# Dot products of units 4 and 5 read the normed rows from SBUF instead of PSUM

## The chip, the cores and the metric

The kernel runs on one core of one Trainium2 chip. The metric is the device time of one execution in microseconds. Three runs of the kernel before took 4679.68, 4685.80 and 4688.55 us; their median is 4685.8 us.

## What is computed

One inference step of a two-layer backbone over two request groups: 128 context tokens (group 0) and 512 latent tokens (group 1). Each layer has a mixing half (an input projection, a gated linear recurrence and an attention, an output projection) and an expert half (PEER), which is the one that matters here. For each token the expert half picks 128 rows of a table `u` (8 heads of 16), takes their dot products with the normed token, and sums 128 rows of a table `v` with the resulting weights:

```
def peer(h, w_q, sub_keys, u, v):
    def block(xb):
        ...
        idx = jnp.take_along_axis(cand_i, best_pos, axis=-1)
        gate = jax.nn.softmax(best_s, axis=-1)
        ue = u[idx]
        act = jax.nn.gelu(jnp.einsum('td,thkd->thk', xb, ue).astype(jnp.float32), approximate=False)
        ve = v[idx]
        return jnp.einsum('thk,thkd->td', (gate * act).astype(xb.dtype), ve)
```

All is float32, and rows have 1024 elements.

## The kernel before

**Units.** The expert half is done in ten units of 128 tokens, numbered `u` = 0 to 9: unit 0 is the context tile of layer 0, units 1 to 4 are the four latent tiles of layer 0, unit 5 is the context tile of layer 1, units 6 to 9 the latent tiles of layer 1. A unit has two stages. In the *u stage*, 128 gathers each bring one row of table `u` for each of the 128 tokens (128 x 4 KB, 512 KB) into one of the ten slots of `ring`, and the vector engine (DVE) takes one dot product with each (`dots`, L1549 to L1557: 64 steps of two). In the *v stage*, 128 gathers bring rows of `v`, and the tensor engine (PE) sums them into `acc` in PSUM (L972). `gelu` stands between the stages, and `finish` (L1566) behind the v stage adds the result to `x`.

**Who issues what.** GpSimd (POOL) issues all gathers, in the order of the units, as indirect DMAs at L679. It waits until the slot has been read: by the dot ten places before (semaphore `gu`), or by the sum (`gv`). SyncE (SP) issues the weight tiles of 512 KB (L616) into `wring`, which has three slots; it waits until the tile three places before has been used.

**Order.** Each engine runs one fixed list of steps, `plan()` (L186), and skips the steps in which it has no part. While a unit does its dots, other work of the plan is spread between them. Beside the dots of unit 4 stand `norms(3, 0) + projections(3, 0)`: the input projection of three latent tiles of layer 1, 26 weight tiles (PE at L757 for the first 12, L763 for the other 14), each evicted from one of two PSUM buffers by ScalarE (ACT), with a DVE step at the end, `fgate` (L1291, L1294), that waits for the last eviction. `norms` are three DVE steps (L1269 to L1281), after 4, 10 and 16 dots. Beside the dots of unit 5 stand the same for the fourth tile, then the recurrence of that tile, which is mostly DVE work. DVE works in order, so a dot that the plan puts behind `fgate` waits for it.

**The operand of the dots.** ACT writes the normed rows of a unit into `h2`, two slots of 128 x 1024 in SBUF (L1041), ahead of the unit. At the start of each unit the step `("hp", u)` makes ACT copy them in two halves into `acc` in PSUM (`normed_rows`, L1190 to L1197). The first half waits for `xh` and the second for `xr`, which `finish` of the unit before raises when `acc` is free. The first dot waits for both copies (L1552). The dot is one custom DVE instruction with two tensor inputs, a slot of `ring` in SBUF and `acc` in PSUM; its 128 x 1024 product is written back to the slot and its sum is read out by a short second instruction.

Of the kernel before, what the change touches and what calls it, by code (L numbers as in the profile page):

```python
# [7 lines left out]
ALU = mybir.AluOpType  # L8
# [17 lines left out]
U0 = [sum(NT[:p]) for p in range(4)]  # L26
NU = sum(NT)
H, DK = 8, 64
QL, KVL, ROPE, DQ = 384, 256, 32, 96
SCALE = float(64 + 32) ** -0.5  # L30
NK, TOPK = 128, 16
# [13 lines left out]
MERGED = 5  # L45
LV = len(LEVELS) + 2
SHARED = {(1, 2), (3, 2)}
BATCHES = [[(0, 1)], [(0, 4)], [(0, 1)], [(0, 3), (3, 4)]]


# [14 lines left out]
def modulations(l, lo, hi):  # L65

    out = []
    for j in range(lo, hi):
        out.append((("ada", l, j), 1.5))
        if j % (3 * SECT) == 2 * SECT - 1:  # L70
            out.append((("adafin", l, j // (3 * SECT)), 1))
    return out


def norms(p, b):

    return [(("norm", p, t, 0), 8) for t in range(*BATCHES[p][b])]


def projections(p, b, lo=0, hi=N_IN):  # L80

    t0, t1 = BATCHES[p][b]
    out = [(("inp", p, b, j), 2 * max(1, (t1 - t0) * 0.9)) for j in range(lo, hi)]
    if hi == N_IN:
        out.append((("fgate", p, b), 4))
        out += [(("small", p), 0)] if b == 0 else []
        out += [(("rows", p), 0), (("latn", p), 3 + 3 * NT[p])] if b == len(BATCHES[p]) - 1 else []
    return out


def scans(p, t0, t1):

    return [(("hg", p, t, m), 4) for t in range(t0, t1) for m in range(LV)]
# [26 lines left out]
def served(p, t):  # L120

    return (t, t + 1) if (p, t) in SHARED else (t,)

# [13 lines left out]
def queries(p, t):  # L137

    return joined(p, t) + searched(p, t)
# [16 lines left out]
def spread(a, b, until=1.0):  # L156

    def placed(steps):
        total, at, out = sum(us for _, us in steps), 0.0, []
        for step, us in steps:  # L160
            out.append(((at + us / 2) / total, step))
            at += us
        return out

    merged = sorted([(x, 0, i, step) for i, (x, step) in enumerate(placed(a))]
                  + [(x * until, 1, i, step) for i, (x, step) in enumerate(placed(b))])
    return [step for _, _, _, step in merged]


def spread_pairs(a, b):  # L170

    return [(step, 3) for step in spread(a, b)]
# [10 lines left out]
    return spread(out + [heads[H]], beside), [(("u", u, c), 1) for c in range((H - 2) * share, NCU)]  # L183


def plan():  # L186

    def alone(steps):
        return [step for step, _ in steps]

    out = alone(modulations(0, 0, 2 * SECT) + norms(0, 0) + projections(0, 0))
    out += spread(scans(0, 0, 1), modulations(0, 2 * SECT, 3 * SECT))
    out += spread(keys_values(0) + spread_pairs(attention(0, 0), outputs(0)), modulations(0, 3 * SECT, N_ADA))
    out += alone([(("keys", 0), 0)] + opened(0))
    entry = {0: (0, 0, norms(1, 0) + projections(1, 0, 0, 20)), 1: (1, 0, attention(1, 1) + joined(1, 1)), 6: (3, 0, attention(3, 1) + joined(3, 1))}
    ahead = {1: spread_pairs(attention(1, 0), outputs(1)) + [(("keys", 1), 0)] + opened(1)}
    prompt_q = queries(2, 0)
    beside_u = {0: projections(1, 0, 20) + scans(1, 0, 1), 1: searched(1, 1)[:-2],
                2: spread_pairs(attention(1, 3), modulations(1, N_ADA // 2, N_ADA)) + queries(1, 2),
                3: keys_values(2) + spread_pairs(attention(2, 0), outputs(2)) + [(("keys", 1), 0), (("score", 1, 3, 0), 3), (("score", 1, 3, 1), 3)],  # L200
                4: norms(3, 0) + projections(3, 0),
                5: norms(3, 1) + projections(3, 1) + scans(3, 3, 4) + keys_values(3)[:6],
                6: searched(3, 1)[:-2], 7: attention(3, 3) + joined(3, 2)}
    beside_v = {0: scans(1, 1, 4) + keys_values(1),
                1: queries(1, 1)[-2:] + spread_pairs(choice(1, 1), spread_pairs(modulations(1, 0, N_ADA // 2), attention(1, 2))),
                2: spread_pairs(choice(1, 2), norms(2, 0) + projections(2, 0, 0, 20)) + projections(2, 0, 20)
                + scans(2, 0, 1),
                3: [(("keys", 2), 0)] + spread_pairs(choice(1, 3), prompt_q[:-2]) + prompt_q[-2:] + choice(2, 0),
                4: scans(3, 0, 3),
                5: keys_values(3)[6:] + spread_pairs(attention(3, 0), outputs(3)) + [(("keys", 3), 0)] + opened(3),  # L210
                6: queries(3, 1)[-2:] + spread_pairs(choice(3, 1), attention(3, 2)), 7: searched(3, 2) + choice(3, 2),
                8: [(("score", 3, 3, 0), 3), (("score", 3, 3, 1), 3)] + choice(3, 3),
                9: [(("y", u), 3) for u in range(NU - 5, NU - 1)]}
    dense = {0: 0.85, 5: 0.85}
    for u in range(NU):
        out += alone(ahead.get(u, []))
        rest = [(("u", u, c), 1) for c in range(NCU)]
        if u in entry:
            steps, rest = chosen_and_read(*entry[u])
            out += [("hp", u)] + steps  # L220
        else:
            out.append(("hp", u))
        out += spread(rest, beside_u.get(u, []), dense.get(u, 1.0))
        out.append(("gelu", u))
        out += spread([(("v", u, c), 1) for c in range(NCV)], beside_v[u], dense.get(u, 1.0))
        out.append(("fin", u))
    return out + [("y", NU - 1)]
# [15 lines left out]
def same_batch(p, t, other):  # L243

    return any(t0 <= t < t1 and t0 <= other < t1 for t0, t1 in BATCHES[p])

# [93 lines left out]
def after(step, name):  # L340

    return TALLY[PLACE[step] + 1].get(name, 0)
# [46 lines left out]
def build(nc, A, O):  # L389
    with ExitStack() as ctx:  # L390
# [6 lines left out]
        def sem(name):  # L397
# [49 lines left out]
        h2 = sb("h2", [P, 2, D])  # L447
# [46 lines left out]
        dot = sb("dot", [P, H * TOPK])  # L494
# [3 lines left out]
        acc = ps("acc", [P, D])  # L498
# [20 lines left out]
        C = {name: sem("s_" + name) for name in (  # L519
            "it",  # L520
            "ia",
            "id",
            "tp",
            "te",
            "td",
            "wu",
            "mods",
# [42 lines left out]
        def normed_home(p, t):  # L570

            return mT2 if (p, t - 1) in SHARED else mT

        def query_home(p, t, half):

            if (p, t - 1) in SHARED:
                return (o, V)[half][:, :, :].rearrange("p a b -> p (a b)")[:, 512:1536].rearrange("p (a t) -> p a t", t=P)
# [23 lines left out]
        def _(sp):  # L601
# [3 lines left out]
            for k, step in enumerate(PLAN):  # L605
# [22 lines left out]
                elif name == "rows":  # L628
                    p, = a
                    sp.wait_ge(C["it"], after(("inp", p, len(BATCHES[p]) - 1, N_IN - 1), "it"))  # L630
                    sp.dma_start(qrow[:, :], A["qrow"][PASSES[p][1]]).then_inc(s_row, 16)
# [59 lines left out]
        def _(pe):  # L691
# [55 lines left out]
            def project(k, p, b, j):  # L747
                t0, t1 = BATCHES[p][b]
                if j == 0:
# [252 lines left out]
        def _(act):  # L1002
# [15 lines left out]
            def norm(k, p, t, which):  # L1018
                g, l = PASSES[p]
                if t == 0:  # L1020
                    act.wait_ge(C["mods"], after(("adafin", l, which), "mods"))
                root(k, st[:, 2:3], st[:, 1:2])
                n = before(k, "tp")
                for i in range(2):
                    src = got_t(n + i)
                    for c in range(4):
                        kc = 4 * i + c
                        if which:
                            dst = normed_home(p, t)[:, kc, :]
                        else:  # L1030
                            dst = hT[:, kc, t * P:(t + 1) * P] if t < BATCHES[p][0][1] else hT1[:, kc, :]
                        ins = nc.scalar.activation(dst, src[:, c, :], ACT.Identity, scale=Am[:, l, which, kc, g:g + 1],
                                                   bias=mods[:, l, 3 * which * KC + kc, g:g + 1])
                    ins.then_inc(C["te"], 1)
                if which:
                    u = U0[p] + t
                    if u >= 2:
                        act.wait_ge(C["hp"], 2 * (u - 1))
                    for i in range(2):
                        src = got_t(n + 2 + i)  # L1040
                        copy(h2[:, u % 2, 512 * i:512 * (i + 1)].rearrange("p (c t) -> p c t", t=P), src)\  # L1041
                            .then_inc(C["te"], 1)
# [213 lines left out]
        def _(dve):  # L1256
            v = nc.vector
# [290 lines left out]

            def dots(k, u, c):  # L1549

                if c == 0:
                    dve.wait_ge(C["hp"], 2 * (u + 1))  # L1552
                for i in range(CU):
                    rows = landed(dve, "peer_u", u, c * CU + i)
                    n = c * CU + i
                    v.tensor_tensor_reduce(rows, rows, acc[:, :], 1.0, 0.0, ALU.mult, ALU.add, dot[:, n:n + 1])\  # L1556
                        .then_inc(C["gu"], 1)  # L1557

            def gelu(k, u):
# [137 lines left out]
```

## Time and profile before

| what | value |
|---|---|
| median of three runs | 4685.8 us |
| span of the profiled execution | 5196.0 us (the profile gives no time outside its span) |
| DVE busy | 2863.5 us, 55% |
| of it the dots, L1556 | 1487.5 us, 1280 instructions |
| PE busy | 2947.7 us, 57% |
| POOL busy | 2429.0 us, 47% |
| gathers (software DMA queue) | 1342.34 MB, 68.6% of the 16 DMA engines |
| weights and other loads (hardware queue) | 240.76 MB, 13.3% |

The profile is one execution under the hardware profiler; its times run from the first instruction of the span. It took 510.2 us longer than the median of the timed runs. Tables by stage list, for a stretch of time, how long each engine was busy, the clock granted to PE as a share of full speed, the busy share of the DMA engines, and the rate at which they moved data. In timelines, the text in brackets is how long the engine was idle before the row, and what ended that.

### The profile page before, as it was taken

To read this page: it belongs to the slowest core of one execution; us is meant where nothing else is said; L and a number is where in the kernel's file an instruction comes from. 1 tells how busy PE (TensorE), PEld (TensorE's weight loads), DVE (VectorE), ACT (ScalarE), POOL (GpSimd) and SP (SyncE) were. 2 spreads that over 40 slices of the span, in tenths; PEclk is the share of its full clock that TensorE was granted. 3 is DMA by queue.
4 is the path that set the end of the run, shared out by engine and by line. 5 is a ranking of instruction groups with operands and counts; after the bars stand their busy time and mean duration, and the time that the engine had idled before them with its cause. 6 is when DMAs were issued, how large, how long until landed. Compare 5 with 4: busy or idle time off the path is not lost. (4 is left out here: it accounts for less than half of the span.)

```text
span 5196.0 us, 51262 instructions
## 1 busy us (share of the span) xinstructions
PE 2947.7 (57%) x18894; PEld 1865.7 (36%) x18894; DVE 2863.5 (55%) x7112; ACT 607.1 (12%) x1305; POOL 2429.0 (47%) x2565
## 2 busy tenths in 40 slices
PE   6758667744677576237457643685466467025025
PEld 5545633634435453123136333253432353000000
DVE  1258572289247544776863458326935833873740
ACT  2210121210111011110101110211111110000000
POOL 0024154045354435555653643445446646566665
PEclk9579788656885698568678875786677577556556
DMA  6468477278899879899985987788789989899998
GB/s 213 147 232 337 148 267 269 92 277 333 312 382 360 303 266 367 345 360 369 348 343 195 335 329 243 259 333 326 301 319 359 358 306 361 326 359 366 363 373 330
DMA packets 440728, 1586.38 MB, mean 305 GB/s; under 512 B 54560, under 2 KB 56992, under 8 KB 438688
## 3 DMA queue, kind: packets, MB, share of 16 engines
q0 software_dynamic: 368640, 1342.34, 68.6%
q1 hardware_dynamic: 71840, 240.76, 13.3%
q8 instruction: 152, 2.49, 0.2%
q14 instruction: 96, 0.79, 0.0%
HBM read 1579.47 MB, written 3.44 MB: 305 GB/s over the span
## 5 line engine op out<-in xcount | busy, mean ns | idle before, releaser
L679 POOL DMA_INDIRECT ring<-in_peer_u,eidx x1280 | 1206.6, 943 | 1581.2 <-DVE dot L1556 780.4
L679 POOL DMA_INDIRECT ring<-in_peer_v,eidxT x1280 | 1222.0, 955 | 1162.7 <-PE acc L972 624.1
L1556 DVE CUSTOM_DVE_ANT_0 ring<-ring,acc 128x1024 f32<-128x1024 f32 x1280 | 1487.5, 1217 | 99.5 <-issue 68.8
L972 PE MATMUL acc<-ring,wz 128*32 128x512 f32 x5120 | 872.3, 771 | 356.4 <-DMA ring<-in_peer_v,eidxT 269.0
L972 PEld LDWEIGHTS acc<-ring,wz 128*32 128x32 f32 x5120 | 145.4, 123 | 858.7 <-issue 833.1
L926 PE MATMUL pp<-hT,wring 128*128 128x128 f32 x2560 | 352.5, 295 | 138.1 <-issue 97.0
L926 PEld LDWEIGHTS pp<-hT,wring 128*128 128x128 f32 x2560 | 329.6, 208 | 177.3 <-issue 124.3
L757 PE MATMUL pp<-hT,wring 128*128 128x128 f32 (+2 forms) x960 | 245.2, 419 | 147.8 <-issue 122.1
L763 PE MATMUL pp<-wring,hT 128*128 128x128 f32 (+1 forms) x2240 | 276.2, 284 | 40.2 <-issue 22.5
L763 PEld LDWEIGHTS pp<-wring,hT 128*128 128x128 f32 x2240 | 267.6, 199 | 59.7 <-issue 36.0
L721 PE MATMUL tb<-ident,gl 128*128 128x128 f32 x10 | 4.5, 446 | 436.7 <-DVE gl L1563 409.6
L757 PEld LDWEIGHTS pp<-hT,wring 128*128 128x128 f32 x960 | 157.0, 214 | 245.0 <-issue 213.0
L922 PE MATMUL pp<-wring,hT 128*128 128x128 f32 x1280 | 181.2, 303 | 84.3 <-issue 48.0
L1496 DVE MAX8 v<-lat 128x8 f32<-128x128 f32 x160 | 46.9, 293 | 307.7 <-ACT lat L1012 263.1
L922 PEld LDWEIGHTS pp<-wring,hT 128*128 128x128 f32 x1280 | 171.0, 215 | 99.0 <-issue 59.5
L892 PE MATMUL tb<-U,hT 128*128 128x64 f32 x480 | 101.8, 388 | 163.7 <-ACT hT L1012 128.1
L721 PE MATMUL tb<-ident,xn 128*128 128x128 f32 (+1 forms) x240 | 52.9, 393 | 241.4 <-DVE xn L1281 173.6
L786 PE MATMUL pp<-wqb 64*128 64x128 f32 x1120 | 113.1, 351 | 120.4 <-DVE wqb L1326 97.9
L1291 DVE TENSOR_SCALAR U<-U,omlb,lb 128x128 f32<-128x128 f32 (+2 forms) x40 | 13.4, 409 | 275.2 <-ACT lat L1012 275.2
L721 PEld LDWEIGHTS tb<-ident,gl 128*128 128x128 f32 x10 | 1.7, 174 | 438.9 <-DVE gl L1563 411.2
L786 PEld LDWEIGHTS pp<-wqb 64*128 64x128 f32 x1120 | 96.2, 246 | 174.1 <-issue 171.5
L892 PEld LDWEIGHTS tb<-U,hT 128*128 128x128 f32 x480 | 93.3, 293 | 179.7 <-ACT hT L1012 140.7
(207 smaller groups left out, 3597.9 us busy)
## 6 DMA issues: line engine op xcount, KB each, us to landing
wring<-in_w_q SPq DMA_DIRECT2D x128, 512.0 KB
wring<-in_w_in SPq DMA_DIRECT2D x125, 512.0 KB
wring<-in_w_ada SPq DMA_DIRECT2D x96, 512.0 KB
wring<-in_w_out SPq DMA_DIRECT2D x64, 512.0 KB
ring<-in_peer_u,eidx POOLq DMA_INDIRECT x1280
ring<-in_peer_v,eidxT POOLq DMA_INDIRECT x1280
wkvb<-in_keys SPq DMA_DIRECT2D x5, 1024.0 KB
wqb<-in_wqb SPq DMA_DIRECT2D x4, 1152.0 KB
```

Of the source, the lines that this page charges most:

```text
L679: pool.indirect_dma_start(ring[:, n % GR, :], None, A[table], bass.IndirectOffsetOnAxis(ap=rows, axis=0),).then_inc(s_g[n % GR], 16)
L721: ins = nc.tensor.transpose(tb[0:m, n % 2, i * P:(i + 1) * P], piece, ident[:, :])
L757: ins = nc.tensor.matmul(out[:, 0:n], wt[:, c, :], h[:, c, 0:n], start=(c == 0), stop=(c == KC - 1))
L763: ins = nc.tensor.matmul(out[:, (t - t0) * P:(t - t0) * P + m], h[:, c, (t - t0) * P:(t - t0 + 1) * P], wt[:, c, 0:m], start=(c == 0), sto ...
L786: ins = nc.tensor.matmul(out[:, e * 512 + gg * P:e * 512 + (gg + 1) * P], KX[r, m % 2, gg, :], QP[r, m % 2, gg, :], start=True, stop=True)
L892: ins = nc.tensor.matmul(tb[:, bank, 256:256 + DK], cols[:, hi, a, :], vatt[:, a, hh * DK:(hh + 1) * DK], start=(a == 0), stop=(a == kt_n ...
L922: project_chunk(p, t, i, "id", lambda out, w, m, c: nc.tensor.matmul(out, m, w, start=(c == 0), stop=(c == KC - 1)))
L926: project_chunk(p, t, i, "ia", lambda out, w, m, c: nc.tensor.matmul(out, w, m, start=(c == 0), stop=(c == KC - 1)))
L972: ins = nc.tensor.matmul(acc[32 * q:32 * q + 32, half * 512:(half + 1) * 512], wz[:, at:at + 32], row[:, half * 512:(half + 1) * 512], sta ...
L1291: ins = v.tensor_scalar(f, f, omlb[:, d, l, a:a + 1], lb[:, d, l, a:a + 1], ALU.mult, ALU.add)
L1496: link(v.max(vals[:, 0:8], src))
L1556: v.tensor_tensor_reduce(rows, rows, acc[:, :], 1.0, 0.0, ALU.mult, ALU.add, dot[:, n:n + 1])\
```

## The change

The step `("hp", u)` is left out of the plan for the units in `DIRECT`, 4 and 5. Their dots take `h2[:, u % 2, :]` as second operand instead of `acc`, and their first dot waits for the ACT steps that write `h2`, through `te`. Since `hp` no longer counts every unit, waits on it go through `after(("hp", ...), "hp")`. The slot of `h2` that a direct unit used is written again for unit 6 or 7, and ACT now waits there until all dots of unit 4 or 5 are done.

```
+DIRECT = (4, 5)
...
+def opening(u):
+
+    return [] if u in DIRECT else [("hp", u)]
...
-            out += [("hp", u)] + steps
+            out += opening(u) + steps
         else:
-            out.append(("hp", u))
+            out += opening(u)
...
-                    if u >= 2:
-                        act.wait_ge(C["hp"], 2 * (u - 1))
+                    if u >= 2 and u - 2 in DIRECT:
+                        act.wait_ge(C["gu"], H * TOPK * (u - 1))
+                    elif u >= 2:
+                        act.wait_ge(C["hp"], after(("hp", u - 2), "hp"))
...
-                if c == 0:
-                    dve.wait_ge(C["hp"], 2 * (u + 1))
+                p = max(q for q in range(4) if U0[q] <= u)
+                if u in DIRECT:
+                    h = h2[:, u % 2, :]
+                    if c == 0:
+                        dve.wait_ge(C["te"], after(("norm", p, u - U0[p], 1), "te"))
+                else:
+                    h = acc[:, :]
+                    if c == 0:
+                        dve.wait_ge(C["hp"], after(("hp", u), "hp"))
...
-                    v.tensor_tensor_reduce(rows, rows, acc[:, :], 1.0, 0.0, ALU.mult, ALU.add, dot[:, n:n + 1])\
+                    v.tensor_tensor_reduce(rows, rows, h, 1.0, 0.0, ALU.mult, ALU.add, dot[:, n:n + 1])\
```

## Rows read from the trace of the kernel before

**Rows 1.** The page's first line, the span.
```profile
span 5196.0 us, 51262 instructions
```
**Rows 2.** Table by stage: stretch, length, busy PE, PEld, DVE, ACT, POOL, clock, DMA, GB/s.
```profile
2516.00:2545.00 29.00, 5.35 (x23) 4.55 (x24) 26.46 (x50) 8.01 (x22) 15.50 (x17) 0.50 0.78 261
2545.00:2690.00 145.00, 57.55 (x131) 31.02 (x129) 125.50 (x215) 7.00 (x16) 96.42 (x103) 0.68 1.01 398
2690.00:2790.00 100.00, 99.17 (x736) 89.88 (x736) 1.87 (x5) 10.73 (x22) 6.56 (x7) 0.96 0.44 140
...
3016.00:3083.00 67.00, 14.89 (x84) 13.84 (x82) 55.69 (x94) 3.80 (x12) 44.95 (x48) 0.58 1.00 399
3083.00:3131.00 48.00, 41.73 (x336) 39.87 (x336) 0.00 (x0) 8.51 (x24) 0.00 (x0) 0.97 0.70 223
3131.00:3251.00 120.00, 39.43 (x329) 36.58 (x328) 114.51 (x235) 11.23 (x19) 52.62 (x56) 0.53 0.73 255
```
**Rows 3.** Timeline of DVE, the step behind which the last dots of unit 4 stand; unit 5.
```profile
2789.99 3.21 DVE L1291 TENSOR_SCALAR U<-U,omlb,lb 128x384 f32<-128x384 f32 x8 [98.13 <-ACT lat L1012]
...
3131.35 2.14 DVE L1291 TENSOR_SCALAR U<-U,omlb,lb 128x128 f32<-128x128 f32 x8 [55.70 <-ACT lat L1012]
```
**Rows 4.** Timeline of PE through the u stage of unit 4 (16 matmuls are one tile).
```profile
2547.69 18.66 PE L757 MATMUL pp<-hT,wring 128*128 128x384 f32 x48 [2.14 <-ACT hT L1032]
2582.76 7.86 PE L757 MATMUL pp<-hT,wring 128*128 128x384 f32 x16 [16.41 <-issue]
...
2690.50 22.38 PE L757 MATMUL pp<-hT,wring 128*128 128x384 f32 x64 [11.17 <-issue]
2712.72 76.95 PE L763 MATMUL pp<-wring,hT 128*128 128x128 f32 x672
```
**Rows 5.** Timelines at the start of unit 4: ACT's second copy, the first dot.
```profile
2515.45 0.60 ACT L1012 ACTIVATE acc<-h 128x512 f32<-128x512 f32 x1 [1.40 <-DVE x L1578]
...
2516.18 1.22 DVE L1556 CUSTOM_DVE_ANT_0 ring<-ring,acc 128x1024 f32<-128x1024 f32 x1 [0.76 <-DVE x L1578]
```
**Rows 6.** Instructions by source line: duration in ns, least, median, most.
```profile
L1556 DVE CUSTOM_DVE_ANT_0 ring<-ring,acc x1280: 1203/1217/1223, 339.1 to 4997.2; 128x1024 f32<-128x1024 f32 x183
...
L1269 DVE CUSTOM_DVE_ANT_0 xn<-x x20: 1218/1220/1275, 46.3 to 4216.7; 128x1024 f32<-128x1024 f32 x20
...
L1311 DVE TENSOR_TENSOR wkvb<-wkvb x70: 691/693/765, 126.6 to 3219.1; 128x512 f32<-128x512 f32 x70
...
L679 POOL DMA_INDIRECT ring<-in_peer_u,eidx x1280: 932/937/1520, 320.5 to 4988.6; - x183
```
**Rows 7.** Timelines of DVE and POOL: gathers that start inside an L1269.
```profile
2520.76 1.22 DVE L1269 CUSTOM_DVE_ANT_0 xn<-x 128x1024 f32<-128x1024 f32 x1
2521.90 0.08 DVE L1269 DVE_READ_ACCUMULATOR2_ANT st<- 128x1 f32 x1
...
2521.41 1.38 POOL L679 DMA_INDIRECT ring<-in_peer_u,eidx  x1 [0.30 <-issue]
...
1242.17 1.22 DVE L1269 CUSTOM_DVE_ANT_0 xn<-x 128x1024 f32<-128x1024 f32 x1
1243.32 0.08 DVE L1269 DVE_READ_ACCUMULATOR2_ANT st<- 128x1 f32 x1
...
1242.68 1.52 POOL L679 DMA_INDIRECT ring<-in_peer_u,eidx  x1 [0.30 <-issue]
```
**Rows 8.** Table by stage of L679 alone: stretch, length, POOL busy, clock, DMA, GB/s.
```profile
2516.00:2690.00 174.00, 111.92 (x119) 0.65 0.97 375
...
4456.00:4619.00 163.00, 110.33 (x118) 0.50 0.97 372
```
**Rows 9.** Timelines at the end of unit 5's u stage: two gathers, the last dot.
```profile
3252.87 0.94 POOL L679 DMA_INDIRECT ring<-in_peer_u,eidx  x1 [1.10 <-DVE dot L1556]
...
3264.05 0.94 POOL L679 DMA_INDIRECT ring<-in_peer_u,eidx  x1 [0.31 <-DVE dot L1556]
...
3273.07 1.22 DVE L1556 CUSTOM_DVE_ANT_0 ring<-ring,acc 128x1024 f32<-128x1024 f32 x1
```

## The prediction

> **What bounds the kernel now.** I read the span first [rows 1]: 5196.0 us, 510.2 us over the median of the timed runs. So every sum below is made on the profiled execution and brought to the timed runs at the end, and that step is the weakest of the working.
>
> Then the table by stage around the two u stages that change [rows 2]. Unit 4 has three parts. From 2516 to 2545 DVE does 16 dots and the three norms. From 2545 to 2690 the DMA engines are full (share 1.01, 398 GB/s), DVE does dots for 125.50 of 145 us, and PE is busy for only 57.55 us at a granted clock of 0.68, though 26 tiles of projection are its only work. From 2690 to 2790 no dots run, the DMA rate is down to 140 GB/s, and PE is busy for 99.17 of 100 us at 0.96, so nearly always at its upper level. In tiles it is the same [rows 4]: three tiles at once when the operand is ready at 2547.69, then one tile in about 22 us (2582.76 is 16.41 us late), then from 2690.50 on 64 matmuls in 22.38 us and 672 in 76.95 us, which is 5.5 to 5.6 us for a tile of 16 or 48. The last two dots stand behind the step that waits for the last of these tiles; DVE idles 98.13 us before it [rows 3]. So unit 4 ends with PE, and PE is late because it was held for as long as the gathers filled the DMA engines. What holds it, the weight tiles themselves or the hand-over from PE to ACT, I can't tell from the rows; it ends when the gathers do.
>
> Unit 5 begins alike. PE is busy 14.89 of 67 us to 3083, then 41.73 of 48 us [rows 2], and DVE idles 55.70 us [rows 3]. From 3131 DVE is the bound, busy 114.51 of 120 us.
>
> **Part 1: the copies go.** At the start of unit 4 ACT's second copy takes 0.60 us and the first dot starts 0.76 us after the last DVE instruction of the unit before [rows 5]. Without the copies DVE goes on by itself, as it does between dots: 0.05 us. The gain is 0.7 us, twice: **-1.4 us**, all of it on the path, since norms, projections and gathers follow these dots. ACT is idle around the copies. The wait on `te` is for rows written units ago. The new wait of ACT for all dots of unit 4 or 5 stands where units 6 and 7 are normed, behind those dots in every list: nothing.
>
> **Part 2: the dot itself.** No row shows this dot with `h2`. The nearest is L1269, the same custom instruction on 128x1024 with both inputs in SBUF: median 1220 ns against 1217, most 1275 [rows 6]. Its two inputs are the same rows; L1311 has two different SBUF tensors and takes 693 ns for 512 columns, a little over half of 1220. The bounds are 0 and +58 ns a dot. I take +3 ns on the 76 dots in the part of unit 5 that DVE bounds: +0.2 us; the upper bound is 76 x 0.058 = +4.4 us. The other dots have idle time behind them.
>
> The Trainium skill ("Vector Engine (DVE) Microarchitecture Reference", Points that are easy to get wrong) says that an instruction of the two-source family with two non-bf16 SBUF sources runs at half throughput. By it the dots would double; the row says 3 ns. The rival below has its price.
>
> **Part 3: what the dot does to POOL.** This decides. A gather takes POOL 937 ns, whatever dot runs beside it; the longest took 1520 [rows 6]. The timelines show who lengthens it [rows 7]. An L1269 ran from 2520.76, its read-out from 2521.90; a gather that started inside it at 2521.41 took 1.38 us and ended at 2522.79, 0.89 after 2521.90. Another started at 1242.68, took 1.52 and ended at 1244.20, 0.88 after 1243.32. So a gather reads something right after its start, stands until a DVE instruction with two SBUF inputs is over, and then needs its remaining 0.89 us. Every dot of units 4 and 5 becomes such an instruction. By this trace a gather asks again 1.24 us after it was let through: the 0.89 that remain, 0.30 between two gathers, and the 0.05 of its 937 ns that lie ahead of the reading. Back-to-back dots end every 1.14 us, as read-outs stand 1.14 to 1.15 behind their starts [rows 7]. It misses the first end and takes the second: one gather in 2.28 us. When dots are further apart than 1.24 us it gets through at each one.
>
> The Trainium skill ("SBUF — State Buffer", Who interferes with whom) has this contention for a GpSimd instruction that reads SBUF, and there the trace agrees. It adds, as an inference, that such DVE operations don't stall descriptor generation; the two gathers above speak against that.
>
> **Part 4: what slower gathers are worth.** In unit 4 the pace lies between 1.24 and 2.28 us; I take the middle, 1.76, since the ring empties, dots then wait for landings, and POOL finds gaps. 116 gathers from 2517.7 take 204 us; with 5 us to land and be used (an estimate between nothing and the 8.1 us between the last gather's end and the last dot [rows 9]), dot 126 is done at 2727. In that time gathers move 524 KB in 1.76 us, 298 GB/s, and of the 398 GB/s there are 100 left, a tile in 5.2 us: as fast as PE takes them. PE alone would be done at 2547.7 + 144 = 2692. So the later one, 2727, sets `fgate`, where 2790 stands now: **-62 us**. The bounds are 0 (the flood stays) and -97 (PE alone decides). No cost hides here: up to 2790 the gathers could have a pace of 2.3 us.
>
> The norms of unit 4 stand after 4, 10 and 16 dots. Ten rows are in the ring, and rows 11 to 16 have from 2517.7 to 2534 to arrive: no delay, bound +2 us.
>
> In unit 5, 52 gathers and 26 tiles have to move before 3131: 78 x 512 KB at 399 GB/s are 102 us, so 3111 at best. Bounds -20 and 0, taken **-10 us**. At its end 10 gathers take 11.2 us from the first start to the last, and the last dot is 8.1 us behind the last gather [rows 9]. At 2.28 they would take 20.5 us, 9.3 more, at 1.76 15.8, 4.6 more; of the 8.1 some is landing. Bounds 0 and +9, taken **+2 us**.
>
> Sum on the profiled execution: -1.4 + 0.2 - 62 - 10 + 2 = -71 us, so a span of 5125 us.
>
> **To the timed runs.** They are 510 us shorter, and PE standing still in a full DMA stretch is just what a profiler could lengthen. I bound the gain of part 4 by all (-72) and nothing, and take half, having no row for either: -36. With -1.4 + 0.2 + 2 this gives -35, so **4650 us**.
>
> **Rivals.**
> *No change (4684 us).* Dots of unit 4 that wait for landings come 1.4 us apart where gathers alone run (118 in 163 us at 372 GB/s [rows 8]), above 1.24, so POOL gets through at each and the flood stays as it is. Left are the 1.4 us. For it: the flood has that pace already (118 in 174 us in unit 4 [rows 8]). Against: DVE is busy 125.50 of 145 us with them [rows 2], so most follow each other at once. Or the hold on PE isn't there in the timed runs, and pace costs nothing.
> *Slower: the gathers become the bound (4720 us).* If in timed runs PE isn't held, unit 4 takes what 118 gathers and 26 tiles need, 144 x 1.31 = 189 us. Gathers decide from 189 / 118 = 1.6 us on. At 1.76 they take 208 (+19), at 2.28 269 (+80), at 1.9 224: +35. For it: the 510 us. Against: the idle 98 us of the profile. Place: u stage of unit 4.
> *Slower: the dot halves its rate (4786 us).* By the page above: +1.07 us on 74 dots from 3131, on 16 before the third norm of unit 4 and 4 before that of unit 5: +100. Against: the 1220 ns [rows 6].
>
> **How the numbers follow.** Forecast 0.50, no change 0.23, gathers as bound 0.24, halved dots 0.03. A measurement tells about 0.2% (9 us) from no change. Faster 0.50, same 0.23, slower 0.27. Range: down to 4600 (-86, the whole of unit 4 less a little), up to 4716 (the slower rival at 1.76 us, +19, with the bounds of tail and dots, +9 and +4, less 1.4); beyond lie some 0.05 and 0.13.
>
> **What would show it.** In the profile after: L1556 at 1220 ns with `h` in place of `acc` for 256 instructions; gathers of units 4 and 5 at 1.2 to 2.0 us instead of 0.94; DMA share under 1 in unit 4 with PE busy meanwhile; the 98 us before L1291 shrunk to under 40, those of unit 5 to about 45. Wrong it is if gathers stay at 0.94, if PE stays held at a lower gather pace, or if the wait before L1291 goes and DVE waits as long for landings instead.

## The result, and the profile after

The changed kernel took 4699.2 us in the median of 20 runs, the kernel before 4688.9 us beside it, also 20 runs: a ratio of 1.0027, 95% interval 1.0014 to 1.0040. By the ratio it is slower by 13 us (7 to 19; the two medians stand 10 apart), where 4650 us, 36 less than before, had been forecast.

The profiled execution of the changed kernel isn't lengthened. Its page:

```profile
span 4704.4 us, 51256 instructions
...
L685 POOL DMA_INDIRECT ring<-in_peer_u,eidx x1280 | 1283.4, 1003 | 1354.7 <-DVE dot L1571 619.9
...
L1571 DVE CUSTOM_DVE_ANT_0 ring<-ring,acc 128x1024 f32<-128x1024 f32 x1024 | 1201.8, 1217 | 82.7 <-DMA ring<-in_peer_u,eidx 67.3
...
L1571 DVE CUSTOM_DVE_ANT_0 ring<-ring,h 128x1024 f32<-128x1024 f32 x256 | 307.0, 1228 | 69.2 <-DMA ring<-in_peer_u,eidx 66.9
```

L1571 are the dots (L1556 before), L685 the gathers (L679 before). A dot with `h`, which is `h2`, takes 1228 ns in the mean, one with `acc` 1217. In the kernels of the experiments the line numbers shift again by a few. The gathers of table `u` take 1003 ns in the mean; in a profile of before below they take 942. All of that is in units 4 and 5, which is seen when L685 is asked for within one unit (least, median, most, in ns; here u stage 4 and u stage 5):

```profile
L685 POOL DMA_INDIRECT ring<-in_peer_u,eidx x128: 933/1000/1990, 2294.5 to 2505.3; - x128
...
L685 POOL DMA_INDIRECT ring<-in_peer_u,eidx x128: 932/955/1992, 2682.6 to 2947.9; - x128
```

So the gathers are held, as the prediction said. But the table by stage of unit 4 has nothing left of the stretch of 100 us without dots in which DVE idled 98 us [rows 2, 3] (columns as in [rows 2]):

```profile
2315.50:2345.00 29.50, 5.21 (x22) 4.41 (x23) 27.11 (x51) 7.80 (x21) 20.47 (x16) 0.50 0.74 249
2345.00:2522.00 177.00, 144.60 (x868) 117.70 (x866) 140.56 (x232) 19.44 (x38) 136.62 (x111) 0.88 1.02 406
```

The DMA engines are full to the end of the stage, and PE does its 26 tiles in it. That looks like a gain of 76 us against [rows 2], while the time says 13 us lost. The two can't both be read against one profile of before, so the first experiment is a second profile of before.

### The profile page after: what moved, and what is told of

Same layout as the page of the kernel before. It is cut to its first block and busy times, and to the rows that moved or that the text cites. A ratio compares the mean times of both kernels' runs of the same rounds, so it can differ in the third digit from the quotient of the medians.

```text
span 4704.4 us, 51256 instructions
## 1 busy us (share of the span) xinstructions
PE 2857.0 (61%) x18894; PEld 1812.3 (39%) x18894; DVE 2882.9 (61%) x7112; ACT 603.8 (13%) x1301; POOL 2514.2 (53%) x2565
## 5 line engine op out<-in xcount | busy, mean ns | idle before, releaser
L685 POOL DMA_INDIRECT ring<-in_peer_u,eidx x1280 | 1283.4, 1003 | 1354.7 <-DVE dot L1571 619.9
L685 POOL DMA_INDIRECT ring<-in_peer_v,eidxT x1280 | 1230.5, 961 | 813.2 <-PE acc L978 453.6
L1571 DVE CUSTOM_DVE_ANT_0 ring<-ring,acc 128x1024 f32<-128x1024 f32 x1024 | 1201.8, 1217 | 82.7 <-DMA ring<-in_peer_u,eidx 67.3
L978 PE MATMUL acc<-ring,wz 128*32 128x512 f32 x5120 | 857.3, 765 | 360.5 <-DMA ring<-in_peer_v,eidxT 347.2
L978 PEld LDWEIGHTS acc<-ring,wz 128*32 128x32 f32 x5120 | 135.7, 121 | 851.1 <-issue 803.1
L932 PE MATMUL pp<-hT,wring 128*128 128x128 f32 x2560 | 322.4, 287 | 46.7 <-DMA wring<-in_w_q 45.1
L1571 DVE CUSTOM_DVE_ANT_0 ring<-ring,h 128x1024 f32<-128x1024 f32 x256 | 307.0, 1228 | 69.2 <-DMA ring<-in_peer_u,eidx 66.9
L932 PEld LDWEIGHTS pp<-hT,wring 128*128 128x128 f32 x2560 | 307.8, 200 | 80.6 <-DMA wring<-in_w_q 52.2
L769 PE MATMUL pp<-wring,hT 128*128 128x128 f32 (+1 forms) x2240 | 278.8, 288 | 36.4 <-DMA wring<-in_w_in_tail 20.6
L769 PEld LDWEIGHTS pp<-wring,hT 128*128 128x128 f32 x2240 | 271.9, 204 | 54.9 <-DMA wring<-in_w_in_tail 21.9
L763 PE MATMUL pp<-hT,wring 128*128 128x128 f32 (+2 forms) x960 | 232.3, 407 | 22.1 <-DMA wring<-in_w_in 13.5
L763 PEld LDWEIGHTS pp<-hT,wring 128*128 128x128 f32 x960 | 153.2, 211 | 111.1 <-issue 61.0
L928 PE MATMUL pp<-wring,hT 128*128 128x128 f32 x1280 | 164.2, 291 | 33.6 <-DMA wring<-in_w_out 26.2
L928 PEld LDWEIGHTS pp<-wring,hT 128*128 128x128 f32 x1280 | 157.0, 204 | 45.3 <-DMA wring<-in_w_out 30.0
```

The source lines that it names most:

```text
L685: pool.indirect_dma_start(ring[:, n % GR, :], None, A[table], bass.IndirectOffsetOnAxis(ap=rows, axis=0),).then_inc(s_g[n % GR], 16)
L763: ins = nc.tensor.matmul(out[:, 0:n], wt[:, c, :], h[:, c, 0:n], start=(c == 0), stop=(c == KC - 1))
L769: ins = nc.tensor.matmul(out[:, (t - t0) * P:(t - t0) * P + m], h[:, c, (t - t0) * P:(t - t0 + 1) * P], wt[:, c, 0:m], start=(c == 0), sto ...
L928: project_chunk(p, t, i, "id", lambda out, w, m, c: nc.tensor.matmul(out, m, w, start=(c == 0), stop=(c == KC - 1)))
L932: project_chunk(p, t, i, "ia", lambda out, w, m, c: nc.tensor.matmul(out, w, m, start=(c == 0), stop=(c == KC - 1)))
L978: ins = nc.tensor.matmul(acc[32 * q:32 * q + 32, half * 512:(half + 1) * 512], wz[:, at:at + 32], row[:, half * 512:(half + 1) * 512], sta ...
```

## The experiments

In all of them two things are read: the ratio of the times to the kernel before, run beside it, and the length of u stages 4, 5, 8 and 9, from the start of a unit's first dot to the end of its last in the timeline of DVE.

**A second profile of before** (no edit).

> The kernel before, unchanged, profiled a second time. The profile of before that was read for the prediction had a span of 5196.0 us, 507 over the median of its timed runs; the profile of the changed kernel has 4704.4 us, 5 us from its own. Theory (the 98 us were that execution's own): the span is about 4690 us, the u stage of unit 4 takes 189 to 200 us instead of 281.1, PE isn't held while the gathers fill the DMA engines, and DVE idles at most 15 us ahead of fgate instead of 98.13. Rival (the hold on PE belongs to this kernel when dots read PSUM): the u stage of unit 4 keeps some 280 us here too, and other units make up for it.

It took 4689.3 us. The span and the gathers on its page, then the two stretches of unit 4 in its table by stage:

```profile
span 4687.5 us, 51262 instructions
...
L679 POOL DMA_INDIRECT ring<-in_peer_u,eidx x1280 | 1205.7, 942 | 1422.1 <-DVE dot L1556 738.8
```

```profile
2313.50:2343.00 29.50, 5.78 (x24) 4.70 (x24) 26.90 (x50) 8.51 (x23) 15.93 (x17) 0.50 0.78 263
2343.00:2515.00 172.00, 144.99 (x865) 117.60 (x864) 138.43 (x231) 18.67 (x37) 103.72 (x111) 0.89 1.02 413
```

U stage 4 takes 201.0 us, not 281.1, with the DMA engines full and PE not held. That is a little over the 189 to 200 us of the theory. Its timeline of PE:

```profile
2345.26 65.11 PE L757 MATMUL pp<-hT,wring 128*128 128x384 f32 x192 [2.14 <-ACT hT L1032]
2410.20 69.84 PE L763 MATMUL pp<-wring,hT 128*128 128x128 f32 x624
2483.86 10.09 PE L763 MATMUL pp<-wring,hT 128*128 128x32 f32 x48 [3.82 <-DMA wring<-in_w_in_tail]
```

Twelve tiles and fourteen with one wait of 3.82 us ahead of the last, where [rows 4] has one tile in 22 us. Beside this profile the change costs 4.4 us in u stage 4 (205.4) and 8.2 in u stage 5 (254.1 against 245.9). Together that is 12.6 us, of 16.9 between the two spans and 13 by the runs. The split between the two units is rough: where they are left as they were, the profiles of this kind have 201.0 to 201.5 us for u stage 4, but 244.0 to 249.6 for u stage 5.

**Which half of the change costs.** First the dots with `h2`, but copies and their wait kept:

```
-    return [] if u in DIRECT else [("hp", u)]
+    return [("hp", u)]
...
                         dve.wait_ge(C["te"], after(("norm", p, u - U0[p], 1), "te"))
+                        dve.wait_ge(C["hp"], after(("hp", u), "hp"))
```

> Dots of units 4 and 5 read h2 as in the change, but the step hp with its two copies and the wait for them stay. Theory 1 (gathers stand behind dots with two SBUF inputs, and units 4 and 5 are bound by gathers): the whole loss stays, +10 to +15 us against before (the change: +12.6), gathers of units 4 and 5 take 1.2 to 1.3 us in the mean. Theory 2 (the loss comes from the start of the unit: the first dot, the lists or the waits that moved): +0 to +3 us (256 dots longer by 11 ns are 2.8 us at most).

Ratio 1.0037 (1.0023 to 1.0051), +17 us; u stages 209.7 and 249.3. Then the copies gone as in the change, but the dots left at `acc` (so their products are false, and only the time is read):

```
-                    h = h2[:, u % 2, :]
+                    h = acc[:, :]
```

> The other half alone: in units 4 and 5 the copies and their wait are gone as in the change, but the dots read acc with whatever it holds, so the dot products of these two units are left wrong and only the time is read. Theory 1: -1.4 us (0.7 us at the start of each of two units), gathers at 0.94 us; no difference that can be measured. Theory 2 (the start of the unit): +10 us or more.

Ratio 1.0000 (0.9987 to 1.0013); u stages 201.3 and 247.3, gathers at 0.94 us. The whole loss stays without the one half and goes without the other: it is in what the dots read. The 1.4 us of the copies are too small to be seen.

**The same edit where nothing hides it.** `DIRECT = (8, 9)`.

> The same edit for units 8 and 9 in place of 4 and 5. In the profile of the changed kernel the u stages of 8 and 9 take 156.4 and 155.4 us for 128 dots, 1.22 us each: DVE bounds them, dots follow each other at once, and the DMA engines have room. Theory 1 (one gather per two dots when dots are back to back, one per dot when they are further apart than 1.24 us): the pace of gathers rises from 1.28 us to between 1.5 and 1.8, the two u stages take 195 to 230 us each, +80 to +140 us in all. Theory 1b (gathers slip through in idle moments of DVE and only their duration grows): +10 to +40 us. Rival (only the dot's 11 ns): +3 us.

Ratio 1.0077 (1.0053 to 1.0101); the medians stand 31 us apart. U stage 8 takes 172.6 us against 156.5, u stage 9 167.8 against 155.4. The size is that of theory 1b, well under theory 1, and the timelines of DVE and POOL tell why. First the beginning of unit 8:

```profile
4019.64 1.22 DVE L1571 CUSTOM_DVE_ANT_0 ring<-ring,h 128x1024 f32<-128x1024 f32 x1
4020.79 0.08 DVE L1571 DVE_READ_ACCUMULATOR2_ANT dot<- 128x1 f32 x1
...
4021.94 1.22 DVE L1571 CUSTOM_DVE_ANT_0 ring<-ring,h 128x1024 f32<-128x1024 f32 x1
...
4019.69 1.99 POOL L685 DMA_INDIRECT ring<-in_peer_u,eidx  x1 [0.30 <-issue]
4021.98 1.99 POOL L685 DMA_INDIRECT ring<-in_peer_u,eidx  x1 [0.30 <-issue]
4024.27 1.99 POOL L685 DMA_INDIRECT ring<-in_peer_u,eidx  x1 [0.30 <-issue]
```

The gather starts 0.05 us after a dot, stands until that dot's read-out at 4020.79, ends 0.89 later at 4021.68, and the next one comes 0.30 later, again just behind the start of a dot. One gather in 2.29 us. Then, some 12 us on:

```profile
4031.15 1.98 POOL L685 DMA_INDIRECT ring<-in_peer_u,eidx  x1 [0.30 <-issue]
4032.25 1.22 DVE L1571 CUSTOM_DVE_ANT_0 ring<-ring,h 128x1024 f32<-128x1024 f32 x1
...
4033.43 0.94 POOL L685 DMA_INDIRECT ring<-in_peer_u,eidx  x1 [0.30 <-issue]
4034.67 1.26 DVE L1571 CUSTOM_DVE_ANT_0 ring<-ring,h 128x1024 f32<-128x1024 f32 x1 [1.19 <-DMA ring<-in_peer_u,eidx]
4034.67 0.94 POOL L685 DMA_INDIRECT ring<-in_peer_u,eidx  x1 [0.30 <-issue]
...
4035.91 0.93 POOL L685 DMA_INDIRECT ring<-in_peer_u,eidx  x1 [0.30 <-issue]
```

The ring has run empty, dots wait for landings, and in their gaps POOL issues at 0.94 again. The table of L685 by stretch (POOL busy, clock, DMA, GB/s) has 60 gathers in the middle 82 us, and 58 in the last 73, which is 1.26 us apiece:

```profile
4016.00:4034.00 18.00, 14.16 (x8) 0.50 0.61 176
4034.00:4116.00 82.00, 64.02 (x60) 0.50 0.98 367
4116.00:4189.00 73.00, 55.62 (x58) 0.50 1.02 408
```

Before (its second profile, L679) has 13, 66 and 46 in 18, 82 and 57 us, so one in 1.24 us from 4045 on:

```profile
4027.00:4045.00 18.00, 12.18 (x13) 0.50 0.77 280
4045.00:4127.00 82.00, 61.83 (x66) 0.50 1.03 420
4127.00:4184.00 57.00, 43.10 (x46) 0.50 1.03 420
```

So the contention limits itself: a DVE that has to wait for rows leaves gaps in which gathers get through. The loss doesn't end with the ring's lead, though. Gather 17 of unit 8 starts 7.0 us later behind the unit's first dot than in the second profile of before, gather 88 starts 17.9 us later, and gather 127 18.2. So the middle of the stage, where some gathers are still held, costs more than the start, and the u stage grows by 16 us.

**A second set of runs.** The next four ran beside a kernel before that took 5208.5 us (29 runs, 5191.6 to 5225.0) where it had taken 4687.0 (4675.8 to 4694.0). It isn't noise: the first profile of before (5196.0) is of this sort, and the 20 runs of the result are of the other. I call these 5205 to 5208 us the second set, and those of 4685 to 4690 us the first. The six groups of experiments ran on six chips, numbers 0, 2, 6 and 10 in the first set, 11 and 13 in the second. No chip came up twice, so this fits a difference between chips and doesn't prove it.

> The change made in all ten units, copies gone. Theory 1 (the loss in a unit is the lead of its ring plus what it takes to fall into step, 12 to 16 us where gathers and DVE run at the same pace, less where DMA or another engine bounds the stage): 28 us for units 8 and 9, 12 us for 4 and 5, 10 to 16 for 3, 0 to 8 each for the other five: +55 to +85 us. Rival (each gather held for the mean 0.3 us of units 4 and 5, all of it on the path): 1280 x 0.3 = +380 us. Rival (only units near the end have no slack): +40 us.

With `DIRECT = tuple(range(10))` the ratio is 0.9751 (0.9708 to 0.9794), faster by 130 us (107 to 152). I had expected a loss. Its four runs scatter from 5012 to 5105 us, so the size is rough, but all four lie under all 29 of before. U stage 4 takes 206.2 us, against 286.4 in a neighbour that keeps `acc` (below), u stage 5 252.7 against 269.1. That is 97 of the 192 us between these two spans (5010.6 and 5202.5); the rest lies in other stages and is not taken apart here. What the gathers and the tiles do meanwhile is in the DMA view: what each queue moved in 120 us within u stage 4 (packets, MB, share of the engines; q0 carries the gathers, q1 the weight tiles). First the profile of before that the prediction read, from 2560 on; then the second profile of before, from 2360:

```profile
q0 software_dynamic: 12390, 45.11, 94.0%
q1 hardware_dynamic: 843, 3.06, 6.9%
```

```profile
q0 software_dynamic: 10709, 38.98, 79.5%
q1 hardware_dynamic: 3757, 11.10, 23.0%
```

At 0.524 MB a tile, 3.06 MB are six tiles and 11.10 are 21. That looks as if the gathers pushed the tiles aside, and the expectations from here on speak of starved tiles. The trace of the first profile of before says otherwise. These are the end of its first three tiles and the start of the fourth on PE, ACT's evictions of the first three, SP's issue of the fifth tile, and the two queues from 2556 to 2564 and from 2564 to 2582 (SP had issued the fourth tile at 2556.06):

```profile
2559.74 6.61 PE L757 MATMUL pp<-hT,wring 128*128 128x384 f32 x20
2582.76 0.98 PE L757 MATMUL pp<-hT,wring 128*128 128x384 f32 x1 [16.41 <-issue]
...
2556.07 0.49 ACT L1012 ACTIVATE U<-pp 128x384 f32<-128x384 f32 x1 [8.43 <-issue]
2582.12 0.49 ACT L1012 ACTIVATE U<-pp 128x384 f32<-128x384 f32 x1 [25.56 <-issue]
2603.98 0.49 ACT L1012 ACTIVATE U<-pp 128x384 f32<-128x384 f32 x1 [21.37 <-remote]
...
2582.12 0.33 SPq L616 DMA_DIRECT2D wring<-in_w_in  x1
```

```profile
q0 software_dynamic: 748, 2.74, 85.0%
q1 hardware_dynamic: 144, 0.52, 16.0%
...
q0 software_dynamic: 2076, 7.55, 102.5%
```

The fourth tile had moved by 2564, within 8 us of its issue and beside the gathers, and until 2582 no tile was asked for. PE did not start it, since both of its PSUM buffers were full: it had done three tiles by 2566.35, of 5.16 us each once they run, so the second ended at about 2561.2. ACT evicted that one only at 2582.12, 21 us later, and PE started 0.15 us behind the eviction. SP, which waits for the same count of finished tiles (semaphore `it`), issued the fifth tile at the same 2582.12. The third tile was evicted 37.6 us after its end. In the second profile of before an eviction follows the end of its tile at once:

```profile
2358.80 0.49 ACT L1012 ACTIVATE U<-pp 128x384 f32<-128x384 f32 x1 [4.67 <-PE pp L757]
```

So what is late in the second set is the hand-over: PE's count of finished tiles reaches ACT and SP some 20 us or more after the last matmul, and q1 moves little because little is asked of it. Why the count is late beside the gathers, no row shows. In the first set it isn't late, and there was nothing to gain.

The other three of these runs:

```
+                    h = h2[:, u % 2, :] if u in DIRECT and n < 64 else acc[:, :]
```

> Units 8 and 9, copies kept; dots 0 to 63 of each read h2, dots 64 to 127 read acc. Seen so far, all 128 dots with h2: u stages of 172.6 and 167.8 us against 156.5 and 155.4, gathers at 1.99 us (one per two dots) from the first dot until the ten rows of the ring are used up, then mostly 0.94 to 1.2. Theory 1 (the lead of the ring is lost once, early in the unit, and after that dots wait for landings and let gathers through): the first half carries nearly the whole loss, +13 to +16 us in unit 8 and +11 to +14 in unit 9, +24 to +30 in all. Rival (each dot with h2 costs the same wherever it stands): half of it, +14 us in all.

> Units 8 and 9, copies kept; dots 0 to 63 read acc, dots 64 to 127 read h2. Without the edit dots of that half already come 1.24 us apart, at the pace of POOL, so the ring has no lead there. Theory 1: a gather or a few are held until the two paces fall into step, 0 to 4 us a unit, +0 to +8 us in all; median of these gathers 0.94 us. Rival (same cost for each dot): +14 us in all.

Dots 0 to 63: ratio 1.0033 (1.0017 to 1.0049), +17 us, u stages 8 and 9 of 178.5 and 188.4 us where the neighbour that keeps `acc` has 171. Dots 64 to 127 (`n >= 64`): 1.0019 (1.0004 to 1.0033), +10 us, but u stages of 171.7 and 173.5. The profiles say early, while the two intervals overlap. The first one was run again beside 4687.6 us:

> Dots 0 to 63 of units 8 and 9 with h2, a second time, for the set in which the kernel before takes 4690 us and gathers and DVE run at the same pace in units 8 and 9. Beside 5208 us it took +17, with u stages of 178.5 and 188.4 us against 171. Theory 1 (the lead of the ring is lost once, early): beside 4690 us the first half carries nearly the whole loss of the two units, +24 to +30 us. Rival (each dot with h2 costs the same): +14 us.

Ratio 1.0077 (1.0052 to 1.0103), +36 us, as much as for all 128 dots, and a little more than theory 1 had (24 to 30); u stages 174.5 and 177.7. The first half carries the whole loss, and +14 us for an even cost is ruled out.

```
-                if c == 0:
-                    dve.wait_ge(C["hp"], after(("hp", u), "hp"))
+                    if n == 1:
+                        dve.wait_ge(C["hp"], after(("hp", u), "hp"))
+                    h = acc[:, :] if n else h2[:, u % 2, :]
```

> In all ten units the copies stay, and only dot 0 of each unit reads h2; dot 1 waits for the copies, which run beside dot 0 (1.20 us of copies beside 1.22 us of dot, and the first copy already ran before). No gather is issued beside dot 0, since the ring is full until it ends. Theory 1: the 0.7 us at the start of each unit are gained with no gather held: -4 to -7 us, gathers at 0.94 us. Rival (gathers beside the first dot are held as well, or the start of a unit isn't on the path): 0 us.

Ratio 0.9989 (0.9975 to 1.0003), -4 us between the medians: of the expected size, but not told from nothing. Its u stages 4 and 5 are 286.4 and 269.1.

**The change in both sets.**

> The change itself, again. The runs so far fall into two sets by how the DMA engines divide their time when gathers keep them full. In the first set the kernel before takes 4676 to 4694 us; in unit 4 the hardware queue, which carries the weight tiles, gets 11.10 MB in 120 us beside the gathers, and PE isn't held. In the second it takes 5192 to 5225 us, the hardware queue gets 2.62 MB in the same 120 us, and u stage 4 takes 286 us, as in the profile read for the prediction (281). Theory (what the change is worth depends on that): beside a before of about 4690 us it is slower by 8 to 18 us again; beside a before of about 5205 us the slower gathers leave room for the tiles, u stage 4 falls from 285 to about 206 us, u stage 5 by 5 to 20, and the change is faster by 60 to 110 us. Rival (the change costs or gains the same in both sets): slower by 8 to 18 us in either.

First set again (4689.9): ratio 1.0031 (1.0015 to 1.0047), u stages 208.4 and 250.1. Unit 4 alone, `DIRECT = (4,)`:

> The change in unit 4 alone. Theory: beside a before of 4690 us +4 to +8 us; beside 5205 us -60 to -85 us, nearly the whole gain. Rival (the gain or loss spreads evenly over units 4 and 5): half of what the change gives in the same set.

1.0005 (0.9991 to 1.0019), u stage 4 of 207.1, 5 of 246.0.

> The change itself a third time, for the set of runs in which the kernel before takes about 5205 us, should it come up. Theory (as for the second time): beside a before of 5205 us -60 to -110 us, u stage 4 at about 206 us with the hardware queue moving some 10 MB in 120 us beside the gathers in place of 2.62; beside a before of 4690 us +8 to +18 us. Rival: +8 to +18 us in either.

This came beside 5206.8 us: 5150.5, ratio 0.9907 (0.9869 to 0.9945), **faster by 48 us** (29 to 68), so the sign of the theory, but less than its 60 to 110. The profiled execution has 5117.7 us, 78 less than the first profile of before. U stage 4 takes 210.2 us, u stage 5 249.2; PE isn't held any more (its lines L763 and L769 are L757 and L763 before), ACT evicts each tile as it ends, and the tiles move at the pace of the first set (120 us from 2570):

```profile
2549.84 64.77 PE L763 MATMUL pp<-hT,wring 128*128 128x384 f32 x192 [2.14 <-ACT hT L1038]
2614.45 69.84 PE L769 MATMUL pp<-wring,hT 128*128 128x128 f32 x624
```

```profile
q0 software_dynamic: 10774, 39.24, 80.0%
q1 hardware_dynamic: 4197, 10.77, 22.5%
```

**Is it the pace of the gathers?** The kernel before with one wait more, dots from `acc`, nothing read from `h2`:

```
+                if table == "peer_u" and u == 4 and col >= 40:
+                    pool.wait_ge(C["it"], after(("inp", 3, 0, (col - 40) * 24 // 88), "it"))
```

> The kernel before, dots from acc and copies in place, but POOL holds the gathers of unit 4 back by a wait: gather n (n from 40 on) waits until PE is through with projection tile (n - 40) x 24 / 88. No dot reads h2. Theory (tiles are starved by gathers that run ahead, and anything that slows the gathers gives the tiles their share): beside a before of 5205 us u stage 4 falls from 285 to 200 to 215 us, -65 to -85 us, gathers at 0.94 us; beside 4690 us the wait never decides, 0 us. Rival (the gain comes from the dots or copies of the change, not from the pace of gathers): 0 us in both sets, or slower because POOL waits as well.

> The kernel before with the gathers of unit 4 held back by PE's progress, a second time and for the same reason. Theory (tiles are starved by gathers that run ahead): beside a before of 5205 us -65 to -85 us, u stage 4 at 200 to 215 us with gathers at 0.94 us; beside 4690 us 0 us, as measured. Rival: 0 us in both sets.

First set 1.0005 (0.9990 to 1.0021). Second set 5124.5 us, ratio **0.9850** (0.9827 to 0.9873), -78 us. U stage 4 is 204.7 us there, with gathers at 0.94, and q1 moves 10.50 MB in its 120 us. So PE is released by holding the gathers back, in either of two ways, and the wait does it without the loss of the change. It isn't that the DMA engines get a rest: they move 419 GB/s in those 120 us, against 402 in the first profile of before. The rows of the first profile of before above say what is released: the late hand-over. Ahead of the held gathers it is still there (the second tile, which ended at about 2554.5, is evicted at 2565.10). That the tiles lacked room on the DMA engines isn't borne out.

**Which reads hold a gather.** Units 8 and 9 with the gathered row as both inputs:

```
+                    v.tensor_tensor_reduce(rows, rows, rows if u in DIRECT else acc[:, :], ...
```

> Units 8 and 9: the dots take the gathered row as both inputs and read neither h2 nor acc, copies kept; so these dot products are left out of the computation and replaced by squares of the rows, and only the time is read. Theory (any DVE instruction with two SBUF inputs holds a gather, whatever the tensor): gathers of 1.99 us, one per two dots, from the first dot until the ring has lost its lead, as with h2; the u stages of 8 and 9 grow by 10 to 18 us each. Rival (it is h2 itself, its place in SBUF or its neighbours): gathers at 0.94 us and no difference.

Ratio 1.0104 (1.0079 to 1.0130); gathers of up to 1.99 us at the start, u stages 185.2 and 168.1. It isn't `h2`, it is the second input in SBUF. Why unit 8 loses 29 us here and 16 with `h2` stays open: its gathers take 1.07 to 1.26 us in the mean of each eight from number 40 to its end, while those of unit 9 are back at 0.95 from number 48 on. When the two paces fall into step is not settled.

**A version against both.** The wait for unit 4, one like it for gathers 36 to 63 of unit 5, and dot 0 alone from `h2` in all units.

> A version that could beat both kernels: dots from acc; gathers of unit 4 held back by PE's progress as in the paced kernel, those of unit 5 from 36 on likewise, up to 63; and in all units dot 0 alone reads h2, with the copies beside it. Theory: beside a before of 4690 us neither wait decides and the starts give 3 to 7 us, -3 to -7 us; beside 5205 us -78 for unit 4 as measured, -15 to -30 for unit 5 (DVE idle 53 us ahead of its fgate there), -4 for the starts: -95 to -115 us. Rival (tiles of unit 5 aren't starved by the gathers): -80 us beside 5205.

> The paced version a second time, for the set in which the kernel before takes about 5205 us. Beside 4685 us it took 4683.1, no difference that can be measured. Theory: beside 5205 us -78 for unit 4 as measured, -15 to -30 for unit 5, -4 for the starts: -95 to -115 us. Rival (tiles of unit 5 aren't starved by the gathers): -80 us.

Twice 0.9994 (0.9978 to 1.0010, and 0.9975 to 1.0014), both in the first set. No difference from before can be measured, and it is faster than the change there; in the second set it has no run, so its gain for unit 5 stays open.

## Why the prediction was wrong

*Part 1, the copies (-1.4 us).* In the profile after, the first dot of unit 4 starts 0.03 us behind the last instruction of the unit before (2314.49 + 1.39 to 2315.91), where [rows 5] has 0.76. Right, and below what a run can tell.

*Part 2, the dot.* 1228 ns against 1217 to 1218, +10 where +3 was taken and +58 was the bound. The rival of halved dots is dead. (Its price counted 74 dots from 3131, where the sum of this part rightly has 76; that is 2 us of the 100.) The Trainium skill ("Vector Engine (DVE) Microarchitecture Reference", Points that are easy to get wrong) has one instruction format at half throughput when both sources are non-bf16 and in SBUF; whether the dot is of that format no run shows, but its 1228 ns show no halving.

*Part 3, the gather.* The mechanism was right to the hundredth: stands until the read-out, 0.89 more, then one in 2.28 us (2.29 measured). Wrong was the middle, 1.76, as a lasting pace. Unit 8 with `h2` has seven held gathers at its start and then one in 1.37 us over 82 us and one in 1.26 over the last 73. In u stage 4 they came 1.61 us apart in the mean with the change and 1.55 in the second profile of before. The text had named that the ring empties, but made a mean of the two paces where the one follows the other in time. The Trainium skill ("SBUF — State Buffer", Who interferes with whom) infers of `tensor_tensor`, a DVE operation that can have both inputs in SBUF, that it doesn't stall descriptor generation; the gathers of 1.99 us beside this dot speak against carrying that over to indirect ones.

*Part 4, the gain.* In the second set it holds in its main lines: u stage 4 fell by 71 us (281.1 to 210.2; -62 was taken), u stage 5 by 18 (-10), the span by 78 (-71). `fgate` of unit 4 started 202.5 us after the first dot (at 2720.69), where 210.8 had been worked out. The gathers came 1.64 us apart there, not 1.76, and the runs have 48 us (29 to 68) and not 78, so the agreement of the span with the sum is in part luck. That PE is held for as long as the gathers run unchecked is borne out by the paced kernel. The choice between weight tiles and hand-over to ACT, left open then, closes on the hand-over: the fourth tile had moved by 2564, and ACT's eviction at 2582.12 started PE. So the 100 GB/s that slower gathers were to leave for the tiles are not what frees PE; that step of the working was wrong in its reason, though the tiles did then move at 90 GB/s (10.77 MB in 120 us).

*To the timed runs: here it failed.* The step that failed is the last one: the gain of part 4 was taken at half, -36 us, for runs in which PE wasn't held, so that this gain was 0 and the change cost 13 us instead. The sum was halved "having no row for either". A row wasn't needed: the timed runs stood 510 us under the profile, and a hold on PE that costs 98 us in one stage [rows 3] is the first candidate for that difference. Half a mechanism was a mean over two cases and occurs in neither: where the hold exists the gain is 48 us by the runs, where it doesn't the gain of part 4 is nothing and the change loses 13. The supposed cause, a profiler that lengthens, was wrong as well. The second profile of before lies within 2 us of its own time, and in the second set runs and profile agree at about 5200.

*The rival that came true* is "the gathers become the bound", with its place in the u stage of unit 4, and its condition, PE not held. It took +35, for a pace of 1.9 us, and had +19 for 1.76. Measured are +4 to +9 us in u stage 4 (205.4, 208.4, 209.7 against 201.0) and +3 to +8 in u stage 5 (254.1, 250.1, 249.3 against 245.9), of which the lower two lie near the 244.0 to 249.6 us of profiles with unit 5 unchanged. The size was off by the same pace: in the full stretch after 2345 the gathers come 1.59 us apart with the change (111 in 177 us) and 1.55 before (111 in 172 us), and the DMA engines are full in both (1.02), so little is left to lose.

*What would show it.* Dots at 1228 ns came, and longer gathers (1218 and 1276 ns in the mean of units 4 and 5, though half of them still took 1.00 us or less). So did the short idle time ahead of `fgate`, none in unit 4 and 12 us in unit 5 (timeline of DVE, after):

```profile
2807.58 2.14 DVE L1299 TENSOR_SCALAR U<-U,omlb,lb 128x128 f32<-128x128 f32 x8 [11.97 <-ACT lat L1018]
```

But it is no sign of the change: the second profile of before has none in unit 4 and 12.6 us in unit 5. The DMA share did not fall under 1 (1.02).

## What to carry to other kernels

Before a trace is priced, hold its span against the timed runs; when they differ by 11%, find the stage and the mechanism that make the difference, and price the change once with it and once without it, never in between. A DVE instruction with two SBUF inputs delays indirect gathers, here at worst to one in two dots (2.29 us), but a ring that runs empty gives most of the pace back, so the cost stays bounded: 12 to 29 us for a stage of 128 gathers where DVE and gathers have the same pace, 4 to 9 where the DMA engines bound the stage. A queue's small share of the bytes doesn't say that its transfers are starved: look when they are issued, when they have moved, and what the consumer's start waits for. Where a consumer is held beside unchecked gathers, try a wait that ties the gathers to its progress: it cost nothing that could be measured where there was no hold (1.0005, 0.9990 to 1.0021) and gave 1.5% where there was one.

## What the hardware showed beside that

The same kernel took 4690 us in the runs of one set and 5205 in those of the other, with profiles that agree. Beside full gather traffic PE's finished tiles were seen by ACT and SP at once in one and 21 us late and more in the other, so that 21 tiles moved in 120 us in the one and six in the other. Of the 508 us between the two profiles of before, u stages 4 and 5 have 101; the rest lies in the other stages (first dot of unit 2 to first dot of unit 3: 530 against 463 us). Without any tiles the gathers were slower too: 420 GB/s in unit 8 (above) against 372 [rows 8], and u stages 8 and 9 of 156 against 171 us. What differs between the sets, the chip, where the tables lie in memory or something else, no run here shows: each chip was met once, and all kernels of a group shared one. Timed runs of the change in the second set scatter more (5119 to 5178) than those of before (5191 to 5222), and I have no cause for it.
